# The values' last conv pieces done later and by the vector engine alone, and a thirteenth seven-product group, in a hybrid mixer layer

## The chip, the core and the metric

The kernel runs on one core of a Trainium2 chip. The metric is the device time of one execution in microseconds: the median of three runs. A profiled execution is a further one, with its own time. The engines are PE (TensorE, matrix products), DVE (VectorE), ACT (ScalarE), POOL (GpSimd, which here mostly issues transfers) and SP (SyncE, which here issues the weights' transfers). Each engine works through its own list of instructions in order and meets the others only at semaphores.

## The reference, cut to what matters

One layer: x of 256 tokens by 4096 is normed and multiplied by one large matrix; the columns of the product feed three mixers, and a second matrix takes the mixers' output back to 4096 columns.

```python
h = rms_norm(x, norm_g)
proj = einsum('bsd,dn->bsn', h, w_in)        # 4096 x about 13000
(aq, ak, av, ai, af, ao, az, bcq, bk, bv, bki, bwi, bz, cqkv, cb, ca, cz) = split(proj)
y_a = ...                                     # chunked mLSTM
y_b = ...                                     # sparse attention
qkv = silu(causal_depthwise_conv(cqkv, d_conv_w))   # 3072 channels, 4 taps
q_c, k_c, v_c = split(qkv, 3)
q_c, k_c = l2_normalize(q_c), l2_normalize(k_c)     # v_c is not normed
y_c = ...                                     # gated delta rule on q_c, k_c, v_c
x = x + einsum('bsm,md->bsd', concat(y_a, y_b, y_c), w_out)
```

The change concerns the six blocks of 512 columns of `cqkv` (the conv columns): their matrix product, the conv and silu behind it, and the move of `v_c` into another layout.

## The kernel before, in words

**Chunks.** The weights are streamed in 536 chunks, numbered in the order in which PE takes them; a chunk holds two row blocks of 128 of one block of 512 columns. fp32 products are made of three fp32r products: every weight tile is split into a high part (ACT, `split_hi`, L1626) and a low part (DVE, `split_lo`, L2021), and PE multiplies high by high, high by low and low by high. A plain chunk is 2 row blocks x 2 token halves x 3 = 12 matmuls of 512 columns. ACT and DVE work three chunks ahead of PE (`AHEAD`); there are four buffers for raw and four for split weights. SP issues the transfer of chunk c when DVE is through with the low part of chunk c-4 (`weights`, L874); for the second chunk of a group (below) it waits for the group's sums instead.

**Seven-product groups.** Conv columns 2 to 5 are worked in two pairs of column blocks (kind `cpair`). For some row-block pairs (`SEVEN`, token `S` in `CONV_ORDER`) the 2x2 block product is made with seven products instead of eight: PE does 6 matmuls in the first chunk (`seven_first`) and 15 in the second (`seven_second`), 21 instead of 24. In exchange DVE makes four sums of raw weights (`seven_sums`, L2031 to L2036), and splits them (ACT L1624, DVE `seven_lo` L2045, two halves). The activations' own sums are made beforehand (`xs`, `xh`, `xl`), one set per row-block pair in `X_S`. When a pair's groups are through, `evs` (DVE, four additions), `evx` (ACT, scaling) and `evn` (DVE, once per column block) bring the seven results together.

**Slots.** A planner (`plan`, L129) lists beside each chunk the pieces of other work that every engine does right after that chunk's own work: the slot. An engine whose list has a piece in slot c does it after its part for chunk c (DVE and ACT: after the split of chunk c+3), in the order in which the planner put pieces into that slot. The pieces that matter here:

- `cd` i (DVE, L2237): turns a conv piece (two of the 24 blocks of 128 channels) after POOL has moved its 32x32 blocks through DRAM (L993, L999), which POOL starts after `evn`; `conv` i: the first tap is a scaled copy on ACT (L1734), the other three taps are six multiply-adds on DVE (L2248); `csil` i (ACT, L1741): the silu. `CONV_SLOTS` gives the slots of the three. Pieces 0 to 7 are queries and keys, 8 to 11 the values.
- `csq` i: ACT squares a piece of queries or keys and splits it (L1747, L1750), DVE makes the low part (L2262); `cn` i: PE sums it over channels with two matmuls (L1379, L1380), waiting for the DVE part; `ce` i: ACT makes the scale, DVE applies it (L2270, L2272). ACT's `csq` waits for all twelve silus.
- `g1` to `g4`, `gb`: the gates' row work, on ACT and DVE (L2173 to L2199), read by PE in slot 130.
- `vd` (DVE, L2258): turns the values after POOL has moved them through DRAM (L1010, L1015). Before, POOL does this right after the conv moves and DVE turns them in slots 133 and 135.
- `cl` (DVE, slots 155 to 191): a triangular solve in lanes, whose operands POOL loads just ahead of it (L1054, L1058).

The last `cpair` chunk is 95; chunks 96 to 111 are the gates' columns, and so on.

Of the kernel before, what the change touches and what calls it, by code (L numbers as in the profile page):

```python
# [16 lines left out]
ALU = mybir.AluOpType  # L17
# [3 lines left out]
P = 128  # L21
D = 4096
SEQ = 256
M = SEQ // P
# [66 lines left out]
def lane_steps():  # L91

    pieces, spent = {}, 0
    for j in range(BLK - 1, 0, -1):
# [12 lines left out]
            [15, 8, 4, 9, 5, 10, 6, 11, 7, 12, 0, 13, 1, 14, 2, 3]]  # L107
SEVEN = [[0, 1, 2, 3, 4, 5], [0, 1, 2, 3, 4, 5],
         [8, 9, 10, 11, 12, 13], [8, 9, 10, 11, 12, 13, 14], [8, 9, 10, 11, 12, 13, 14]]
Y_S = [8, 9, 10, 11, 12, 13, 14]  # L110
OUT_PAIRS = range(2, 5)
CONV_SINGLE = 2
CONV_ORDER = ["12S1111S11S1122S22S22S1222", "12S11S11S11S11S22S12222222"]
X_S = [0, 1, 2, 3, 4, 5]
CONV_SLOTS = [(33, 34, 35), (35, 37, 39), (38, 43, 45), (46, 51, 53), (72, 78, 79), (75, 87, 89),
              (80, 91, 91), (82, 94, 94), (97, 99, 100), (99, 104, 105), (104, 105, 107), (106, 108, 109)]
CSQ_FROM = 110
PAIR_SLOTS = [(59, 60, 62, 63), (88, 89, 89, 97)]
S_PIECES = [(8, 10, 11), (9, 18, 23), (12, 25, 28), (17, 26, 30), (18, 34, 42), (25, 40, 44), (46, 47, 54)]
# [9 lines left out]
def plan():  # L129
# [77 lines left out]
    def weave(at, pieces, every=1):  # L207

        for piece in pieces:
            woven[at] += [] if piece is None else piece if isinstance(piece, list) else [piece]  # L210
            at += every
        return at
# [33 lines left out]
    at = max(weave(at + 1, [("ce", i) for i in range(8)]), g_end)  # L246
    weave(g_end + 1, [("vd", 0), ("vd", 1)], 2)
    weave(at + 4, [("kn", 0), ("kr", 0), ("kd", 0), ("kx", 0)], 3)
# [65 lines left out]
def hybrid_kernel(nc, x, norm_g, w_in, w_out, m_ib, m_fb, m_norm_g, a_cq_g, a_wuq, a_wuqi, a_qn_g, a_kn_g,  # L314
# [13 lines left out]
    with ExitStack() as ctx:  # L328
# [611 lines left out]
        def _(pool):  # L940
# [65 lines left out]

            pool.wait_ge(conv_ready, 12)
            for hg in range(2):
                for i in range(4):
                    pool.dma_start(v_dram[hg].rearrange("a f j i b -> i a (f j) b")[i],  # L1010
                                   v_heads(hg)[32 * i:32 * i + 32].rearrange("p (f b) -> p f b", b=32)
                                   ).then_inc(v_kept, 16)
                pool.wait_ge(v_kept, 16 * 4 * (hg + 1))
                for j in range(4):
                    pool.dma_start(v_heads(hg)[32 * j:32 * j + 32].rearrange("p (f c) -> p f c", c=P),  # L1015
                                   v_dram[hg][:, :, j].rearrange("a f i b -> a f (i b)")).then_inc(v_moved[hg], 16)

            wait_read(pool, "cn", 7)
# [38 lines left out]
            for g in range(LANE_G):  # L1057
                pool.dma_start(lane_left[lane_part(g)].rearrange("p r c -> p (r c)"),  # L1058
                               lane_left_dram[:].rearrange("m s k r c -> (m s k) (r c)")
                               ).then_inc(lane_left_loaded, 16)  # L1060
            pool.wait_ge(v_kept, 16 * 8 * M)
            for j in range(4):
# [535 lines left out]
        def _(act):  # L1598
# [129 lines left out]

            def conv(i, use):
                wait_read(act, "par", 0, 1)  # L1730
                act.wait_ge(conv_turned, i + 1)
                for j in range(2):
                    c = 2 * i + j
                    ins = func(cT[:, c, :], conv_columns(i, j), ACT.Copy,  # L1734
                               scale=par[:, R_N + 3 * CH + c:R_N + 3 * CH + c + 1])
                ins.then_inc(conv_y, 1)
# [6 lines left out]
            def csq(i, use):  # L1743
                act.wait_ge(conv_ready, 12)
                if i >= 2:
# [254 lines left out]
        def _(dve):  # L2000
# [241 lines left out]
            def conv(i, use):  # L2242
                dve.wait_ge(conv_y, i + 1)
                for d in range(1, CONV_K):
# [420 lines left out]
```

## Time and profile before

| | us |
|---|---|
| median of 3 runs | 1515.25 (1514.6 to 1515.85) |
| profiled execution | 1515.99 |
| its span, first to last instruction | 1514.1 |
| PE busy in it | 1509.8 |
| DVE busy | 1138.6 |
| ACT busy | 821.5 |
| POOL busy | 367.0 |

The profile's page gives busy time by engine, the groups of instructions, the chain of work that ended last and the transfers. The trace behind it can be asked for every instruction of a stretch (the timeline, with the idle time of the engine before an instruction in brackets and what ended it), for the waits of an engine, for the busy time in given stretches (windows) and for a stretch of the chain. Times are counted from the span's start. Matmuls are pipelined and the end of each is modelled, so the distance from one start to the next tells PE's pace, and not the duration given.

### The profile page before, as it was taken

The numbers are of one execution on the slowest core, as the hardware profiler recorded it, in microseconds if no ns is written. First come the engines' busy times: TensorE is split into PE (matmuls) and PEld (weight loads), VectorE is DVE, ScalarE is ACT, GpSimd is POOL, SyncE is SP. The second block draws the span as 40 slices with busy tenths as digits, with TensorE's granted clock in tenths as the row PEclk, the third lists the DMA queues.
The fourth block names the chain that finished last, engine by engine and source line by source line (L and its number), as shares of the span: only waits on it lengthen the run. The fifth ranks groups of instructions, "written<-read, shape, count | busy, mean of one in ns | idle before, by whom it ended". The sixth has DMA issues, their size and how long they took to land.

```text
span 1514.1 us, 19057 instructions
## 1 busy us (share of the span) xinstructions
PE 1509.8 (100%) x6900; PEld 1249.9 (83%) x6900; DVE 1138.6 (75%) x1712; ACT 821.5 (54%) x1100; POOL 367.0 (24%) x612
## 2 busy tenths in 40 slices
PE   9999999999999999999999999999999999999999
PEld 7888888888888887888878888888888888888887
DVE  6889899847769855576579676676557789988894
ACT  6766656587533444554545545544345656555563
POOL 9040131330230040126420254344400112000101
PEclk9999999999999999999999999999999999999999
DMA  9876677976788775558765787798875667696867
GB/s 288 283 238 218 198 250 209 254 225 195 223 252 267 235 221 165 158 184 271 248 203 167 231 248 205 241 277 241 236 244 158 216 217 221 205 263 210 237 228 187
DMA packets 209070, 341.47 MB, mean 226 GB/s; under 512 B 53161, under 2 KB 60632, under 8 KB 208720
## 3 DMA queue, kind: packets, MB, share of 16 engines
q1 hardware_dynamic: 184784, 288.66, 61.2%
q0 software_dynamic: 24144, 51.57, 13.1%
q8 instruction: 55, 0.90, 0.2%
q14 instruction: 39, 0.32, 0.1%
q10 hardware_dynamic: 48, 0.02, 0.0%
HBM read 312.81 MB, written 30.83 MB: 227 GB/s over the span
## 4 chain that ended last, share of the span: by engine, by line
PE 98%; DVE 1%; ACT 0%; issue 0%; DMA 0%; DVEq 0%
PE acc L1289 25%; PE acc L1292 25%; PE acc L1291 25%; PE mix L1292 2%; PE mix L1291 2%; PE mix L1289 2%; PE mix L1305 2%; PE mix L1307 2%; PE mix L1306 2%; PE acc L1305 2%; PE acc L1307 2%; PE acc L1306 2%; PE mix L1398 1%; PE mix L1481 1%; PE mix L1470 0%; PE mix L1391 0%
## 5 line engine op out<-in xcount | busy, mean ns | idle before, releaser
L2021 DVE TENSOR_TENSOR w_lo<-w_raw,w_hi 128x1024 fp32r<-128x1024 f32 (+1 forms) x503 | 604.0, 1216 | 252.8 <-ACT w_hi L1626 247.9
L1626 ACT ACTIVATE w_hi<-w_raw 128x1024 fp32r<-128x1024 f32 (+1 forms) x503 | 522.5, 1049 | 371.8 <-PE acc L1292 277.3
L1289 PE MATMUL acc<-w_hi,op_hi 128*128 128x512 f32 (+1 forms) x1628 | 640.4, 393 | 0.3 <-DVE w_lo L2021 0.3
L1292 PE MATMUL acc<-w_hi,op_lo 128*128 128x512 f32 (+1 forms) x1628 | 633.4, 389 | 0.0
L1291 PE MATMUL acc<-w_lo,op_hi 128*128 128x512 f32 (+1 forms) x1628 | 633.3, 389 | 0.0
L1289 PEld LDWEIGHTS acc<-w_hi,op_hi 128*128 128x128 f32 x1628 | 305.7, 188 | 64.7 <-issue 1.3
L1292 PEld LDWEIGHTS acc<-w_hi,op_lo 128*128 128x128 f32 x1628 | 305.6, 188 | 63.8
L1291 PEld LDWEIGHTS acc<-w_lo,op_hi 128*128 128x128 f32 x1628 | 305.8, 188 | 61.9
L993 POOL DMA_DIRECT2D conv_dram<-y x48 | 30.7, 703 | 165.6 <-DVE y L2112 118.4
L1289 PE MATMUL mix<-w_hi,op_hi 128*128 128x512 f32 (+1 forms) x154 | 59.7, 388 | 0.0
L1291 PE MATMUL mix<-w_lo,op_hi 128*128 128x512 f32 (+1 forms) x154 | 59.7, 388 | 0.0
L1292 PE MATMUL mix<-w_hi,op_lo 128*128 128x512 f32 (+1 forms) x154 | 59.7, 388 | 0.0
L1624 ACT ACTIVATE t_hi<-t_raw 128x1024 fp32r<-128x1024 f32 x40 | 42.2, 1060 | 16.1 <-DVE t_raw L2031 10.2
L1154 POOL DMA_DIRECT2D bp_dram<-b_ps x48 | 31.4, 701 | 71.7 <-ACT b_ps L1860 66.1
L2045 DVE TENSOR_TENSOR t_lo<-t_raw,t_hi 128x1024 fp32r<-128x1024 f32 x40 | 47.0, 1218 | 0.0
L1617 ACT ACTIVATE w_hi<-w_raw 128x512 fp32r<-128x512 f32 x32 | 20.2, 632 | 48.8 <-PE mix L1307 21.5
L993 POOL DMA_DIRECT2D y_dram<-y x32 | 21.0, 831 | 98.3 <-DVE y L2367 68.6
L1860 ACT ACTIVATE b_ps<-b_s,st 128x128 f32<-128x128 f32 (+1 forms) x32 | 14.3, 446 | 45.6 <-DVE st L2488 45.6
L993 POOL DMA_DIRECT2D bq_dram<-qs x32 | 20.5, 712 | 74.2 <-DVE qs L2415 74.2
L1165 POOL DMA_DIRECT2D b_pT<-bp_dram x48 | 26.4, 566 | 35.7 <-DMA bp_dram<-b_ps 35.7
L1226 POOL DMA_DIRECT2D out_dram<-sum x4 | 4.8, 1443 | 120.6 <-DVE sum L2100 120.6
L1291 PEld LDWEIGHTS mix<-w_lo,op_hi 128*128 128x128 f32 x154 | 28.9, 188 | 6.0
(566 smaller groups left out, 1798.8 us busy)
## 6 DMA issues: line engine op xcount, KB each, us to landing
w_raw<-in_w_in_dram SPq DMA_DIRECT2D x367, 512.0 KB, 4.5
w_raw<-in_w_out_dram SPq DMA_DIRECT2D x128, 512.0 KB, 4.7
w_raw<-in_w_in_dram SPq DMA_DIRECT2D x16, 384.0 KB, 3.8
w_raw<-in_a_wuq_dram SPq DMA_DIRECT2D x12, 512.0 KB, 5.8
out_dram<-acc POOLq DMA_DIRECT2D x8, 512.0 KB, 7.0
out_dram<-in_x_dram POOLq DMA_DIRECT2D x7, 512.0 KB, 6.3
conv_dram<-y POOLq DMA_DIRECT2D x48, 64.0 KB, 4.0
y<-conv_dram POOLq DMA_DIRECT2D x48, 64.0 KB, 4.3
```

The costliest lines, as they stand in the source:

```text
L993: pool.dma_start(*kept_block(dst, src, m, i)).then_inc(signal, 16)
L1154: pool.dma_start(bp_dram[n % 2][:, :, :, i, :].rearrange("a k j b -> a (k j) b"), b_ps[32 * i:32 * i + 32, n % 2].rearrange("p (f b) -> p ...
L1289: nc.tensor.matmul(o, hi[:, kt, tok], hv[:, i, n0:n1], start=(kt == (kts if late else blk["kts"])[0]), stop=False)
L1291: nc.tensor.matmul(o, hi[:, kt, tok], lv[:, i, n0:n1], start=False, stop=False)
L1292: last_mm = nc.tensor.matmul(o, lo[:, kt, tok], hv[:, i, n0:n1], start=False, stop=(kt == blk["kts"][-1]))
L1305: nc.tensor.matmul(o, x_hi, w_hi_, start=start, stop=False)
L1306: nc.tensor.matmul(o, x_hi, w_lo_, start=False, stop=False)
L1307: return nc.tensor.matmul(o, x_lo, w_hi_, start=False, stop=stop)
L1624: func(halves(sum_hi)[:, half], sums[:, half], ACT.Copy).then_inc(t_hi_ready, 1)
L1626: func(split_ap(w_hi, c), w_raw[:, c % RAW_BUFS, 0:n], ACT.Copy).then_inc(hi_ready, 1)
L2021: vec.tensor_tensor(split_ap(w_lo, c), w_raw[:, c % RAW_BUFS, 0:n], split_ap(w_hi, c).bitcast(F32), ALU.subtract).then_inc(lo_ready, 1)
L2045: vec.tensor_tensor(halves(sum_lo)[:, half], sums[:, half], halves(sum_hi)[:, half].bitcast(F32), ALU.subtract).then_inc(t_lo_ready, 1)
```

## The change

The diff does four things. Conv columns 4 and 5 get a seventh seven-product group (thirteen in the conv columns instead of twelve), with one more set of activation sums, and the order of the chunks of both pairs changes a little. The slots of the conv pieces move: queries and keys within slots 31 to 95, piece 8 to 104 to 107, and pieces 9, 10 and 11 to slots 113, 119 and 124, with their silus at 147, 149 and 151. For these three pieces (`DVE_TAPS`) the first tap, too, is done by DVE, as two scalings, and ACT has no tap; ACT's squares wait for eight silus instead of twelve. The values' move through DRAM goes behind POOL's loads for the lane solve, and its turn on DVE from slots 133 and 135 to 195 and 197 (`V_FROM`).

```diff
--- before.py
+++ after.py
@@ -105,17 +105,19 @@
 COPY_FROM, COPY_EVERY = 166, 3
 PAIR_KTS = [[4, 5, 6, 7, 8, 15, 9, 14, 10, 0, 11, 1, 12, 2, 13, 3], [15, 8, 4, 5, 9, 6, 10, 7, 11, 0, 12, 1, 13, 2, 14, 3],
             [15, 8, 4, 9, 5, 10, 6, 11, 7, 12, 0, 13, 1, 14, 2, 3]]
-SEVEN = [[0, 1, 2, 3, 4, 5], [0, 1, 2, 3, 4, 5],
+SEVEN = [[0, 1, 2, 3, 4, 5], [0, 1, 2, 3, 4, 5, 6],
          [8, 9, 10, 11, 12, 13], [8, 9, 10, 11, 12, 13, 14], [8, 9, 10, 11, 12, 13, 14]]
 Y_S = [8, 9, 10, 11, 12, 13, 14]
 OUT_PAIRS = range(2, 5)
 CONV_SINGLE = 2
-CONV_ORDER = ["12S1111S11S1122S22S22S1222", "12S11S11S11S11S22S12222222"]
-X_S = [0, 1, 2, 3, 4, 5]
-CONV_SLOTS = [(33, 34, 35), (35, 37, 39), (38, 43, 45), (46, 51, 53), (72, 78, 79), (75, 87, 89),
-              (80, 91, 91), (82, 94, 94), (97, 99, 100), (99, 104, 105), (104, 105, 107), (106, 108, 109)]
+CONV_ORDER = ["1211S11S11S1122S22S22S1222", "12S11S11S11S12S2222S22S12"]
+X_S = [0, 1, 2, 3, 4, 5, 6]
+CONV_SLOTS = [(31, 40, 41), (31, 43, 45), (42, 53, 55), (49, 57, 59), (71, 77, 79), (77, 81, 83),
+              (77, 85, 86), (86, 93, 95), (104, 106, 107), (109, 113, 147), (110, 119, 149), (112, 124, 151)]
 CSQ_FROM = 110
-PAIR_SLOTS = [(59, 60, 62, 63), (88, 89, 89, 97)]
+DVE_TAPS = 9
+V_FROM = 195
+PAIR_SLOTS = [(59, 61, 61, 64), (93, 94, 94, 97)]
 S_PIECES = [(8, 10, 11), (9, 18, 23), (12, 25, 28), (17, 26, 30), (18, 34, 42), (25, 40, 44), (46, 47, 54)]
 A_SLOTS = [(1, 4, 10), (7, 11, 18), (22, 27, 30), (34, 36, 41)]
 YD_SLOTS = [40, 43, 53, 62]
@@ -244,7 +246,7 @@
         at = weave(at, [([("csq", i)] if i < 8 else []) + ([("cn", i - 2)] if i > 1 else [])])
     g_end = weave(max(at, end("gates", 512) + 2), [(name, 0) for name in ("gt", "g1", "g2", "g3", "g4", "gb")], 2)
     at = max(weave(at + 1, [("ce", i) for i in range(8)]), g_end)
-    weave(g_end + 1, [("vd", 0), ("vd", 1)], 2)
+    weave(V_FROM, [("vd", 0), ("vd", 1)], 2)
     weave(at + 4, [("kn", 0), ("kr", 0), ("kd", 0), ("kx", 0)], 3)
     for u in range(len(UNITS)):
         at = weave(at, [("ca", u), None, ("cg", u), None])
@@ -1004,17 +1006,6 @@
                 pool.wait_ge(conv_kept, 16 * 4 * M * (j + 1))
                 bring_blocks(conv_stage(j), conv_dram[j % 2], brought[j % 2])
 
-            pool.wait_ge(conv_ready, 12)
-            for hg in range(2):
-                for i in range(4):
-                    pool.dma_start(v_dram[hg].rearrange("a f j i b -> i a (f j) b")[i],
-                                   v_heads(hg)[32 * i:32 * i + 32].rearrange("p (f b) -> p f b", b=32)
-                                   ).then_inc(v_kept, 16)
-                pool.wait_ge(v_kept, 16 * 4 * (hg + 1))
-                for j in range(4):
-                    pool.dma_start(v_heads(hg)[32 * j:32 * j + 32].rearrange("p (f c) -> p f c", c=P),
-                                   v_dram[hg][:, :, j].rearrange("a f i b -> a f (i b)")).then_inc(v_moved[hg], 16)
-
             wait_read(pool, "cn", 7)
             clear_corners(1)
 
@@ -1058,6 +1049,17 @@
                 pool.dma_start(lane_left[lane_part(g)].rearrange("p r c -> p (r c)"),
                                lane_left_dram[:].rearrange("m s k r c -> (m s k) (r c)")
                                ).then_inc(lane_left_loaded, 16)
+            pool.wait_ge(conv_ready, 12)
+            for hg in range(2):
+                for i in range(4):
+                    pool.dma_start(v_dram[hg].rearrange("a f j i b -> i a (f j) b")[i],
+                                   v_heads(hg)[32 * i:32 * i + 32].rearrange("p (f b) -> p f b", b=32)
+                                   ).then_inc(v_kept, 16)
+                pool.wait_ge(v_kept, 16 * 4 * (M + hg + 1))
+                for j in range(4):
+                    pool.dma_start(v_heads(hg)[32 * j:32 * j + 32].rearrange("p (f c) -> p f c", c=P),
+                                   v_dram[hg][:, :, j].rearrange("a f i b -> a f (i b)")).then_inc(v_moved[hg], 16)
+
             pool.wait_ge(v_kept, 16 * 8 * M)
             for j in range(4):
                 pool.dma_start(c_kt[32 * j:32 * j + 32],
@@ -1727,6 +1729,8 @@
                 func(gder[:, 2:4, :], gcol[:, 0:2, :], ACT.Exp).then_inc(g_cols, 1)
 
             def conv(i, use):
+                if i >= DVE_TAPS:
+                    return
                 wait_read(act, "par", 0, 1)
                 act.wait_ge(conv_turned, i + 1)
                 for j in range(2):
@@ -1741,7 +1745,7 @@
                 func(t, t, ACT.Silu).then_inc(conv_ready, 1)
 
             def csq(i, use):
-                act.wait_ge(conv_ready, 12)
+                act.wait_ge(conv_ready, 8)
                 if i >= 2:
                     act.wait_ge(c_sq_lo, i - 1)
                 step(func(c_square(i), cT[:, 2 * i:2 * i + 2, :].rearrange("p c t -> p (c t)"), ACT.Square))
@@ -2240,7 +2244,15 @@
                 vec.transpose(part, part).then_inc(conv_turned, 1)
 
             def conv(i, use):
-                dve.wait_ge(conv_y, i + 1)
+                if i < DVE_TAPS:
+                    dve.wait_ge(conv_y, i + 1)
+                else:
+                    dve.wait_ge(conv_turned, i + 1)
+                    for j in range(2):
+                        c = 2 * i + j
+                        row = R_N + (CONV_K - 1) * CH + c
+                        step(vec.tensor_scalar(cT[:, c, :], conv_columns(i, j), par[:, row:row + 1], None, ALU.mult),
+                             but=1 - j)
                 for d in range(1, CONV_K):
                     for j in range(2):
                         c = 2 * i + j
```

## Rows read from the trace of the kernel before

**Rows 1.** The page, part 1: busy us (share) and instructions by engine.

```profile
PE 1509.8 (100%) x6900; PEld 1249.9 (83%) x6900; DVE 1138.6 (75%) x1712; ACT 821.5 (54%) x1100; POOL 367.0 (24%) x612
```

**Rows 2.** Waits of PE, whole span: total us, times, longest.

```profile
PE acc L1289 <- DVE w_lo L2021: 0.3, 1, 0.3
```

**Rows 3.** Timeline of PE, 316.9 to 321: start us, us, what.

```profile
317.04 0.39 PE L1289 MATMUL acc<-w_hi,op_hi 128*128 128x512 f32 x1
...
319.76 0.39 PE L1379 MATMUL mix<-csq_hi,ones 128*128 128x512 f32 x1
```

**Rows 4.** Timeline of DVE, 234 to 240: work of one seven-product group.

```profile
234.44 1.22 DVE L2031 TENSOR_TENSOR y<-w_raw 128x1024 f32<-128x1024 f32 x1
...
237.02 0.69 DVE L2016 TENSOR_TENSOR w_lo<-w_raw,w_hi 128x512 fp32r<-128x512 f32 x1
237.62 2.36 DVE L2045 TENSOR_TENSOR tc_lo<-y,tc_hi 128x1024 fp32r<-128x1024 f32 x2
```

**Rows 5.** Timeline of DVE, 171 to 229 (idle time in brackets).

```profile
171.54 0.69 DVE L2097 TENSOR_TENSOR part_sum<-mix,y 128x512 f32<-128x512 f32 x1 [1.72 <-ACT y L1914]
...
177.74 2.36 DVE L2021 TENSOR_TENSOR w_lo<-w_raw,w_hi 128x1024 fp32r<-128x1024 f32 x2 [2.08 <-ACT w_hi L1626]
...
228.20 2.32 DVE L2045 TENSOR_TENSOR tc_lo<-y,tc_hi 128x1024 fp32r<-128x1024 f32 x2
```

**Rows 6.** Timeline of PE at 232.65: the first matmul of chunk 84.

```profile
232.65 0.39 PE L1289 MATMUL mix<-w_hi,op_hi 128*128 128x512 f32 x1
```

**Rows 7.** Windows: stretch, length, then busy us (instructions) by engine.

```profile
187.00:264.00 77.00, 77.00 (x341) 63.74 (x341) 72.62 (x89) 45.56 (x54) 19.45 (x34) 1.00 0.76 232
413.00:437.00 24.00, 24.00 (x108) 19.94 (x107) 14.15 (x16) 10.17 (x10) 12.74 (x25) 1.00 0.85 238
540.00:560.00 20.00, 20.00 (x90) 16.57 (x89) 9.80 (x8) 8.41 (x9) 9.12 (x12) 1.00 0.90 248
```

**Rows 8.** Timeline of DVE: taps, one-source scalings, value transposes.

```profile
299.18 2.45 DVE L2248 SCALAR_TENSOR_TENSOR cT<-y,par,cT 128x255 f32<-128x255 f32 x6
...
344.90 0.27 DVE L2173 TENSOR_SCALAR rows<-rows 8x256 f32<-8x256 f32 x1
...
377.74 1.30 DVE L2258 STREAM_TRANSPOSE cT<-cT 128x512 f32<-128x512 f32 x2
...
415.03 0.54 DVE L2233 TENSOR_SCALAR kiT<-mix,par 128x256 f32<-128x256 f32 x1
```

**Rows 9.** Timeline of DVE at 316.89: fourth squared piece's low part.

```profile
316.89 0.69 DVE L2262 TENSOR_TENSOR csq_lo<-kv,csq_hi 128x512 fp32r<-128x512 f32 x1
```

**Rows 10.** Timeline of DVE, 349 to 352.3: slot 124.

```profile
349.67 1.21 DVE L2021 TENSOR_TENSOR w_lo<-w_raw,w_hi 128x1024 fp32r<-128x1024 f32 x1
...
351.56 0.69 DVE L2270 SCALAR_TENSOR_TENSOR cT<-cT,c_vk 128x512 f32<-128x512 f32 x1 [0.68 <-ACT c_vk L1758]
```

**Rows 11.** Chain that ended last, 352 to 361.5: start us, us, what.

```profile
352.51 1.22 DVE w_lo L2021
...
354.33 1.14 DVE w_lo L2021
...
360.30 1.15 DVE w_lo L2021
...
361.49 0.50 PE acc L1289
```

**Rows 12.** The page, part 6: weight transfers, KB each, us to landing.

```profile
w_raw<-in_w_in_dram SPq DMA_DIRECT2D x367, 512.0 KB, 4.5
```

**Rows 13.** DMA issues, 300 to 326, with the values' moves under way.

```profile
w_raw<-in_w_in_dram SPq DMA_DIRECT2D x8, 512.0 KB, 4.6
```

**Rows 14.** DMA issues, 425 to 450, lane solve's loads under way.

```profile
w_raw<-in_w_in_dram SPq DMA_DIRECT2D x8, 512.0 KB, 8.1
```

**Rows 15.** Timelines of DVE and PE, 440 to 446: chunk 158.

```profile
442.63 1.22 DVE L2021 TENSOR_TENSOR w_lo<-w_raw,w_hi 128x1024 fp32r<-128x1024 f32 x1 [5.04 <-ACT w_hi L1626]
...
445.89 0.39 PE L1289 MATMUL acc<-w_hi,op_hi 128*128 128x512 f32 x1
```

## The prediction

> **What bounds the kernel now.** I read the page's busy times first: PE is busy 1509.8 us of a span of 1514.1, DVE 1138.6 [rows 1]. Since a matmul's end is modelled, the second view is PE's timeline: from one chunk's first matmul at 317.04 to the work behind it at 319.76 lie 2.72 us for 12 matmuls, 0.227 us each, and this pace holds nearly throughout [rows 3]. The third view is what PE waits for: behind the start there is one wait, 0.3 us for a low part of the weights [rows 2]. So PE is the bound, at its own pace, and a change can do two things: alter the number of matmuls, or make PE wait. PE waits when DVE or ACT delivers a chunk's split, or a piece that PE needs, later than PE gets there. The fourth view is therefore where DVE is nearly full. From 187 to 264 (the second pair of conv columns) it is busy 72.62 of 77 us [rows 7]; and from 352.5 to 361.45 the chain that ended last runs through DVE without a break, up to the low part of chunk 130, for which PE waits [rows 11]. The chain's rows say: there, every microsecond more on DVE is a microsecond more at the end.
>
> **The change part by part.**
>
> The thirteenth group takes away 24 matmuls and adds 21: 3 x 0.227 = 0.68 us less on PE, the whole gain. On DVE a group costs the sums, 237.02 - 234.44 = 2.58 us; a half split, 237.62 - 237.02 = 0.60; and the low parts of the sums, 2 x 1.14 = 2.28, each as long as a split, against one full split of 1.14 that falls away [rows 4, 11]: 4.3 us more on an engine with 77 - 72.62 = 4.4 idle in that stretch [rows 7]. Is there room? In the first pair's end DVE idles 1.72 us before its additions, and then 2.08 before chunk 64's split, because ACT scales before it splits [rows 5]. The new slots put that scaling one slot later, so that DVE splits chunk 64 while ACT scales. Running DVE's list on from there, with one more conv piece ahead of the additions, I get the low parts of the group at chunk 83 to start at 226.8 instead of 228.20 [rows 5]. From 226.8: low parts to 229.1, split 84 to 230.2, six taps (now in slot 81) to 232.6, split 85 to 233.75. Chunk 89's weights are issued then and land 4.5 us later [rows 12], at 238.3; the sums end at 240.9, six taps at 243.3, the half split at 243.9, a turn (half of a pair's 1.30 [rows 8]) at 244.55, the first low half at 245.75. PE: chunk 84 starts at 232.65 [rows 6]; four plain chunks (10.88), six matmuls of the group's first chunk (1.36) and three of its second (0.68) bring it to 245.57. It waits 0.2 us. By the same walk chunks 47, 90, 97 and 98 have 0.5 to 1.1 us to spare, the additions of the second pair included. Bounds: no wait at all, and 1.5 us (rival two). I take 0.2.
>
> The extra activation sums (slots 29 to 31) are six short DVE operations, which I put at a group's sums and a half split, 3.2 us. The first group now begins at chunk 36 instead of 34, and two plain chunks leave DVE 2 x (2.72 - 1.14) = 3.2 us [rows 3, 11]. Hidden; at worst 0.5 us.
>
> A conv piece wholly on DVE is six taps, 2.45 us, and two scalings of 256 elements from SBUF. The trace has no such scaling of 128 partitions; the nearest rows are 0.27 us (256 elements, 8 partitions, SBUF) and 0.54 (128 partitions, but out of PSUM) [rows 8]. I take 0.27, the row with the same memory: 3.0 us a piece, and 3.5 as the upper bound.
>
> Against that choice I set a rule. The Trainium skill (VectorE: DVE Perf Modes, sections on Mode 2×_2P and on why PSUM operands drop a tier) says that an fp32 op with one tensor source runs two elements a cycle in SBUF and loses that with PSUM. By it the 0.54 is no model for the tap, as I assumed; were it one, the sum below would be 1.1 us higher.
>
> Slot 113 holds piece 9 ahead of the fourth squared piece on DVE. The latter starts at 316.89 today, right behind chunk 116's split, which waits for ACT [rows 9]. Queued behind 3.0 us of taps it starts at 319.9 and ends at 320.6. PE wants it in slot 115, when chunk 115 is through, at 319.76 [rows 3]: a wait of 0.85 us. (All in times of before; PE's own shift carries ACT and DVE along there, since they wait for its buffers.) Behind it are queued split 117, which DVE then makes at 320.6 to 321.8, before PE can have done chunk 116 (2.72 behind the wait), and on ACT the sixth piece's square, two slots on. Bounds: 0.5 to 1.4.
>
> Slot 119 holds piece 10. DVE waits for ACT both before and after it there (slots 119 to 121), so I put it at nothing; without that cover it costs its 3.0.
>
> Slot 124 holds piece 11, ahead of `ce3` on DVE. Chunk 127's split starts at 349.67 and takes 1.14, so DVE is free at 350.81; today it idles 0.68 us until ACT hands over `ce3` at 351.56 [rows 10]. The taps end at 353.8, `ce3` at 354.4, and split 128 starts then instead of at 352.51: 1.9 us late, the 3.0 less what the two waits for ACT swallow. From there the chain has no gap [rows 11], and the gates' row work lies in it: split 130 ends 1.9 us later than 361.45, and PE, already waiting for it today, waits 1.9 more. Bounds 1.5 to 2.4. DVE stays that much later until its idle time after 365; POOL's transfers of the gates' rows move with it, as PE does.
>
> ACT loses three pairs of taps and its silus move into 147 to 151, after an exponential, so a table load goes with the first; slot 207's silu then needs none. ACT is busy 10.17 of 24 us there [rows 7]: nothing. Without that cover each silu would cost its length.
>
> The values' move: POOL now issues it behind the lane solve's loads and no longer ahead of the corners' clearing and the gates' rows. Queued behind it on POOL are four loads for slot 209 and copies that wait for chunk 166's split, both late enough for its two round trips. The turns cost DVE 1.30 us a pair [rows 8], and at 195 and 197 DVE is busy 9.8 of 20 us [rows 7]: nothing either way, since PE does not wait at 133 to 135 today. Without cover, 2.6 us. What the transfers do to the weights is rival three.
>
> Sum: -0.68 + 0.2 + 0.85 + 1.9 = +2.27 us. Against the profiled execution (1515.99, of which the span is 1514.1) that is 1518.3; against the median of the runs, 0.74 lower, 1517.5. I forecast **1517.5**, 0.15% over before. About 0.2% (3.0 us) is what a measurement of this kernel can tell from no change, so this counts as no change, close to its edge.
>
> **The rivals.**
>
> One: the taps find room. If the scalings and taps pack tighter, or the two waits are swallowed by leads that I read too small, only the gain is left: 1515.25 - 0.68 = 1514.6; with half the waits, 1515.9. For it: ACT has less to do in 97 to 111. Against it: the wait at 361.49 is there already [rows 11], and DVE's order is fixed.
>
> Two: the second pair is full. Chunk 89's sums wait for its weights, and from there DVE has no idle time up to chunk 90. Place: PE in chunk 89. Price: all that the landing takes over 4.5 us; at 6 us it is 1.5 us, the sum +3.8, **1519.0**, slower. It decides from a landing of about 5.3 us (0.76 more makes 3.0). For it: under the lane loads a landing takes 8.1 us [rows 14], under the values' moves 4.6 [rows 13]. Against it: POOL moves nothing at that time.
>
> Three: the values' move jams the weights of chunks 158 to 161. Today transfers there take 8.1 us in the median [rows 14], chunk 158's low part ends at 443.85, PE starts it at 445.89 [rows 15]: 2.0 us are left. The moves put 0.5 MB in the place of another 0.5 MB and then three more batches over the next 20 us. If the landing of 158 grows by 4 us, PE waits 2: **1519.5**. It costs from 2.0 us of growth on. Against it: with these same moves under way at 300 to 326 a landing took 4.6, one tenth over the usual 4.5 [rows 12, 13].
>
> The Trainium skill (DMA: Bandwidth & Descriptors, section Issuing engines are not separate DMA queues) has all issuers' transfers on the same 16 DMA engines, interleaved, which is what rival three would need; the 8.1 us agree with it.
>
> That the change doesn't do what it says has no place: the matmuls are counted off by the code.
>
> **How the numbers follow.** Forecast 0.55 (its own range 1516.6 to 1518.8: the bounds of its terms), rival one 0.17, two 0.16, three 0.12. The range reaches down to 1515.1, halfway into rival one, and up to 1519.6, over two and most of three. Faster by over 0.2% (under 1512.2) has no mechanism: PE has no wait to lose but 0.5 us; 0.01. Slower (over 1518.28): rivals two and three, 0.28, and about a sixth of the forecast, 0.09; 0.37. The same: 0.62.
>
> **What would show it.** Right: PE 3 matmuls shorter; a gap of some 0.9 us in PE ahead of the two norm matmuls behind chunk 115, and of some 2.4 (0.5 today) ahead of chunk 130, with DVE named as the releaser of both; 8 DVE instructions of 3.0 us in slots 113, 119, 124; no gap at chunk 89 over 0.5, none at 158 to 166. Wrong: no gap at 115 or 130 (rival one), a gap in the second group chunk that waits on tc_lo (two), splits waiting for weights after 440 (three), or DVE scalings of 0.5 us.

## The result, and the profile after

The changed kernel takes 1519.02 us (median of 8 runs) and the kernel before 1515.18 in the same set: a ratio of 1.0025, with a 95% interval from 1.0016 to 1.0034. A second set of ten runs (E0 below) gave 1518.66 against 1515.46, 1.0021 with an interval from 1.0012 to 1.0031. The change makes the kernel 3.2 to 3.8 us slower. That lies on the edge of what counts as no change here (about 0.2%), and more likely just past it.

The profiled execution of after took 1520.24 us, of which the span is 1518.4. The page's first part answers to [rows 1]:

```profile
PE 1510.9 (100%) x6897; PEld 1249.0 (82%) x6897; DVE 1146.4 (75%) x1729; ACT 821.4 (54%) x1097; POOL 368.1 (24%) x612
```

The window of the second conv pair answers to [rows 7]:

```profile
187.00:264.00 77.00, 76.24 (x336) 62.52 (x335) 72.48 (x89) 45.38 (x55) 13.60 (x24) 1.00 0.73 220
```

PE has three matmuls fewer (6897 for 6900), so the group does what it says. In the second pair's stretch PE is no longer busy all the time (76.24 of 77). The view of PE's waits over the whole span, with the total, how often, and the longest, answers to [rows 2]:

```profile
PE acc L1291 <- DVE w_lo L2025: 1.9, 1, 1.9
PE mix L1560 <- DVE kv L2615: 1.1, 1, 1.1
PE acc L1307 <- DVE tc_lo L2049: 0.8, 1, 0.8
PE mix L1381 <- DVE csq_lo L2274: 0.7, 1, 0.7
PE mix L1307 <- DVE t_lo L2049: 0.2, 1, 0.2
```

The second of them belongs to the start and is in before's trace as well. The others are new or have grown, and DVE is the releaser of every one. From here on I measure a wait from start to start on PE's timeline, less the 0.227 us of a matmul at full pace; the bracket in a row leaves out part of it.

The fourth row is the norm matmuls behind chunk 115, against [rows 3, 9]. PE's timeline:

```profile
319.08 0.39 PE L1294 MATMUL acc<-w_hi,op_lo 128*128 128x512 f32 x1
320.16 0.50 PE L1381 MATMUL mix<-csq_hi,ones 128*128 128x512 f32 x1 [0.69 <-DVE csq_lo L2274]
```

1.08 - 0.23 = 0.85 us. DVE's timeline shows why:

```profile
316.40 0.61 DVE L2254 TENSOR_SCALAR cT<-y,par 128x256 f32<-128x256 f32 x2
317.04 2.46 DVE L2260 SCALAR_TENSOR_TENSOR cT<-y,par,cT 128x255 f32<-128x255 f32 x6
319.42 0.68 DVE L2274 TENSOR_TENSOR csq_lo<-kv,csq_hi 128x512 fp32r<-128x512 f32 x1
```

Piece 9 takes 3.02 us from its first scaling to the squared piece, and the squared piece that ran at 316.89 before now starts at 319.42.

The first row is chunk 130, against [rows 10, 11]. PE's timeline, from its last matmul of chunk 129:

```profile
361.62 0.39 PE L1294 MATMUL acc<-w_hi,op_lo 128*128 128x512 f32 x1
363.92 0.50 PE L1291 MATMUL acc<-w_hi,op_hi 128*128 128x512 f32 x1 [1.91 <-DVE w_lo L2025]
```

The chain that ended last runs from slot 124 to it on DVE alone:

```profile
351.40 0.54 DVE cT L2254 x2
...
351.96 2.46 DVE cT L2260 x6
354.42 0.60 DVE cT L2282
355.02 1.14 DVE w_lo L2025
...
362.73 1.15 DVE w_lo L2025
...
363.92 0.50 PE acc L1291
```

The wait is 2.30 - 0.23 = 2.07 us, where before had 0.48 (from 360.78 to 361.49). Another 0.2 us stands ahead of chunk 128.

Behind that wait comes what I had not foreseen. PE's timeline:

```profile
365.25 0.63 PE L1294 MATMUL acc<-w_hi,op_lo 128*128 128x512 f32 x1
365.68 0.63 PE L1291 MATMUL acc<-w_hi,op_hi 128*128 128x512 f32 x1
366.11 0.63 PE L1293 MATMUL acc<-w_lo,op_hi 128*128 128x512 f32 x1
```

The window of the same stretch, after and then before, with the granted clock third from the right (0.64 and 1.00):

```profile
364.00:368.00 4.00, 4.00 (x12) 2.97 (x12) 4.00 (x5) 1.00 (x2) 2.97 (x4) 0.64 0.71 154
...
364.00:368.00 4.00, 4.00 (x25) 3.13 (x24) 2.91 (x6) 1.59 (x3) 1.63 (x3) 1.00 0.84 217
```

From 365.25 to 367.81 the matmuls start 0.427 us apart instead of 0.227: PE runs at the lower of its two levels, 1.2 GHz. The row counts 12 matmuls in these 4 us. From chunk 130's first matmul to chunk 131's are 5.17 us (363.92 to 369.09), 1.6 more than in before (361.49 to 365.08).

The third row is the group of chunk 89, against [rows 4, 6], first in PE's timeline:

```profile
231.63 0.39 PE L1291 MATMUL mix<-w_hi,op_hi 128*128 128x512 f32 x1
...
244.52 0.40 PE L1309 MATMUL mix<-w_hi,s_more 128*128 128x512 f32 x1
245.68 0.50 PE L1307 MATMUL acc<-tc_hi,s_more 128*128 128x512 f32 x1 [0.76 <-DVE tc_lo L2049]
```

Then in DVE's:

```profile
238.25 1.23 DVE L2035 TENSOR_TENSOR y<-w_raw 128x1024 f32<-128x1024 f32 x1 [0.51 <-DMA w_raw<-in_w_in_dram]
...
244.44 2.32 DVE L2049 TENSOR_TENSOR tc_lo<-y,tc_hi 128x1024 fp32r<-128x1024 f32 x2
```

PE waits 1.16 - 0.23 = 0.93 us there.

The lane solve's stretch, against [rows 14, 15]: the weight transfers in the view of DMA issues from 425 to 450.

```profile
w_raw<-in_w_in_dram SPq DMA_DIRECT2D x9, 512.0 KB, 8.1
```

Chunk 158's low part in DVE's timeline, from 445.84 to 447.07 (PE takes it at 449.89):

```profile
445.84 1.23 DVE L2025 TENSOR_TENSOR w_lo<-w_raw,w_hi 128x1024 fp32r<-128x1024 f32 x1 [4.25 <-ACT w_hi L1628]
```

The landing takes 8.1 us as it did, and 2.8 us are left for chunk 158, where 2.0 were.

### The profile page after: what moved, and what is told of

The parts are those of the page before. It is cut to its first block, busy times and chain, and to the rows that moved or that the text cites. A ratio compares the mean times of both kernels' runs of the same rounds, so it can differ in the third digit from the quotient of the medians.

```text
span 1518.4 us, 19065 instructions
## 1 busy us (share of the span) xinstructions
PE 1510.9 (100%) x6897; PEld 1249.0 (82%) x6897; DVE 1146.4 (75%) x1729; ACT 821.4 (54%) x1097; POOL 368.1 (24%) x612
## 4 chain that ended last, share of the span: by engine, by line
PE 91%; DVE 5%; DMA 2%; ACT 1%; issue 1%; SPq 0%; ACTq 0%; DVEq 0%
PE acc L1291 25%; PE acc L1293 25%; PE acc L1294 25%; PE mix L1307 1%; PE mix L1309 1%; PE mix L1308 1%; DVE w_lo L2025 1%; PE mix L1293 1%; PE mix L1291 1%; PE mix L1294 1%; PE acc L1307 1%; PE acc L1308 1%; PE acc L1309 1%; PE mix L1400 1%; DVE cT L2260 1%; PE mix L1483 1%
## 5 line engine op out<-in xcount | busy, mean ns | idle before, releaser
L1294 PE MATMUL mix<-w_hi,op_lo 128*128 128x512 f32 (+1 forms) x146 | 56.6, 388 | 0.0
L1293 PE MATMUL mix<-w_lo,op_hi 128*128 128x512 f32 (+1 forms) x146 | 56.6, 388 | 0.0
L1626 ACT ACTIVATE tc_hi<-y 128x1024 fp32r<-128x1024 f32 x26 | 27.6, 1062 | 16.4 <-DVE y L2035 11.3
```

The costliest lines, as they stand in the source:

```text
L1293: nc.tensor.matmul(o, hi[:, kt, tok], lv[:, i, n0:n1], start=False, stop=False)
L1294: last_mm = nc.tensor.matmul(o, lo[:, kt, tok], hv[:, i, n0:n1], start=False, stop=(kt == blk["kts"][-1]))
L1626: func(halves(sum_hi)[:, half], sums[:, half], ACT.Copy).then_inc(t_hi_ready, 1)
```

## The experiments

Each kernel was timed beside the kernel before on the same chip; E1 to E4 ran on one chip, E0 and E5 to E7 on a second, E8 to E10 on a third, E11 on a fourth. Medians in us, the ratio to before with its 95% interval:

| run | what | median | before | ratio | interval |
|---|---|---|---|---|---|
| E0 | the changed kernel again | 1518.66 | 1515.46 | 1.0021 | 1.0012 to 1.0031 |
| E1 | twelve groups | 1519.88 | 1515.80 | 1.0025 | 1.0015 to 1.0035 |
| E2 | late pieces in 118, 119, 120 | 1515.30 | 1515.80 | 0.9996 | 0.9987 to 1.0005 |
| E3 | in 113, 119, 120 | 1516.63 | 1515.80 | 1.0005 | 0.9996 to 1.0014 |
| E4 | in 118, 119, 124 | 1517.62 | 1515.80 | 1.0014 | 1.0005 to 1.0023 |
| E5 | ACT does the scalings | 1517.62 | 1515.46 | 1.0016 | 1.0007 to 1.0024 |
| E6 | E2, piece 6 later | 1515.57 | 1515.46 | 1.0001 | 0.9992 to 1.0010 |
| E7 | in 118, 123, 124 | 1521.13 | 1515.46 | 1.0040 | 1.0027 to 1.0054 |
| E8 | before, values' move late | 1514.64 | 1515.82 | 0.9994 | 0.9985 to 1.0003 |
| E9 | in 118, 126, 126 | 1523.74 | 1515.82 | 1.0050 | 1.0037 to 1.0062 |
| E10 | E2, key and value factors later | 1514.62 | 1515.82 | 0.9995 | 0.9986 to 1.0004 |
| E11 | E10 and E6 together | 1514.31 | 1515.80 | 0.9991 | 0.9982 to 1.0000 |

**E2, the late pieces where DVE is idle.** Theory: slots 113 and 124 are the cause of the loss. Rivals: the late silus and the values' move are; or the slow stretch has a cause of its own.

```diff
-              ... (109, 113, 147), (110, 119, 149), (112, 124, 151)]
+              ... (109, 118, 147), (110, 119, 149), (112, 120, 151)]
```

> The changed kernel with the taps of pieces 9, 10 and 11 in slots 118, 119 and 120, where its trace shows VectorE idle for 0.8 to 3.9 us at a time, and nothing else changed. My theory: all that the change lost behind chunk 112 comes from where pieces 9 and 11 stand. The 0.85 us at the norm matmuls behind chunk 115 goes, the wait ahead of chunk 130 falls from 2.07 to the 0.49 of before, and the stretch of matmuls 0.427 us apart behind it (364 to 368 us, 1.6 us lost) goes with it, since before had no such stretch there. Together 0.85 + 1.6 + 1.6 = 4.05 less: about 1515.0, within 0.2% of before. Rival one, that the slow stretch has nothing to do with the wait (it belongs to the place or to that execution): only 2.45 less, 1516.6. Rival two, that the late silus or the values' move cost the time: within 0.5 of the changed kernel, 1518.5 to 1519.5.

Measured: 1515.30, 0.5 below before, and all of PE's waits in the trace are these:

```profile
PE mix L1560 <- DVE kv L2615: 1.1, 1, 1.1
PE acc L1291 <- DVE w_lo L2025: 0.3, 1, 0.3
PE mix L1307 <- DVE t_lo L2049: 0.2, 1, 0.2
```

The waits behind chunk 115 and at chunk 128 are gone, that at chunk 130 is back at 0.49 (0.72 from start to start), and so is the granted clock at 1.00. The 3.2 to 3.8 us went with the slots of two pieces; silus at 147 to 151 and the values' move, which this kernel keeps, cost nothing that shows.

**E3 and E4, one of the two pieces at a time.**

```diff
E3:
+              ... (109, 113, 147), (110, 119, 149), (112, 120, 151)]
E4:
+              ... (109, 118, 147), (110, 119, 149), (112, 124, 151)]
```

> The changed kernel with piece 9's taps left in slot 113, piece 10's in 119 and piece 11's moved from 124 to 120. My theory: 0.85 us of wait ahead of the norm matmuls behind chunk 115 stays, the 2.07 us ahead of chunk 130 falls to 0.5 and the half-speed matmuls behind it go: 1519.0 - 1.6 - 1.6 = 1515.8. Rival, the half-speed stretch is not tied to the wait: 1517.4.

> The changed kernel with piece 9's taps moved from 113 to 118, piece 10's in 119, piece 11's left in 124. My theory: only the 0.85 us behind chunk 115 goes; about 2.1 us of wait ahead of chunk 130 stays, and so does the stretch behind it with matmuls 0.427 us apart, 1.6 us: about 1518.2, and 1515.8 + 1518.2 - 1515.0 is the changed kernel again if the two pieces' costs add. Rival, the slow stretch came of both waits together or of that execution: 1516.6.

Measured against E2 on the same chip: E3 is 1.33 above it (the theory had 0.8) and E4 2.32 (the theory had 3.2); together 3.65. The traces split them cleanly. E3's PE timeline has the one wait, 1.08 - 0.23 = 0.85 us again, and chunk 130's is at 0.48:

```profile
319.36 0.39 PE L1294 MATMUL acc<-w_hi,op_lo 128*128 128x512 f32 x1
320.44 0.50 PE L1381 MATMUL mix<-csq_hi,ones 128*128 128x512 f32 x1 [0.69 <-DVE csq_lo L2274]
```

E4's has the other, 2.31 - 0.23 = 2.08, with the slow stretch behind it in the profiled execution (granted clock 0.57 from 364 to 368):

```profile
360.44 0.39 PE L1294 MATMUL acc<-w_hi,op_lo 128*128 128x512 f32 x1
362.75 0.50 PE L1291 MATMUL acc<-w_hi,op_hi 128*128 128x512 f32 x1 [1.92 <-DVE w_lo L2025]
...
364.24 0.61 PE L1291 MATMUL acc<-w_hi,op_hi 128*128 128x512 f32 x1
364.65 0.63 PE L1293 MATMUL acc<-w_lo,op_hi 128*128 128x512 f32 x1
365.08 0.63 PE L1294 MATMUL acc<-w_hi,op_lo 128*128 128x512 f32 x1
```

But the slow stretch isn't in every execution. The mean granted clock was 0.999 in 2 of E4's 11 executions and 1.000 in the others. The median of those that read 1.000 is 1517.53, 2.2 above E2. The mean over a whole execution has three digits, so a fall that costs less than about half of the 1.6 us above would still read 1.000, and only a profiled execution shows where the clock fell. That the falls of the others lie behind chunk 130 too is concluded from the kernels: no execution reads below 1.000 without a wait of 2 us or more there.

**E1, twelve groups.** It isolates the group and asks whether that is what keeps chunk 89 waiting.

```diff
-SEVEN = [[0, 1, 2, 3, 4, 5], [0, 1, 2, 3, 4, 5, 6],
+SEVEN = [[0, 1, 2, 3, 4, 5], [0, 1, 2, 3, 4, 5],
-              "12S11S11S11S12S2222S22S12"]
+              "12S11S11S11S12S2222S221212"]
-X_S = [0, 1, 2, 3, 4, 5, 6]
+X_S = [0, 1, 2, 3, 4, 5]
```

> The changed kernel with the second conv pair back at six grouped pieces, slots and values' move as changed. My theory: the 13th group is worth its three matmuls, 3 x 0.227 = 0.68 us, and has no part in the wait ahead of chunk 89's group matmuls (0.93 us in the changed kernel's trace), since it lies behind it, in chunks 92 and 93. So PE gets three matmuls more, 6900, the 0.93 stays within 0.2, and the time is 0.7 us above the changed kernel, about 1519.7. Rival: the seventh group's sums and splits are what made VectorE late; then the 0.93 goes, and the time is 0.2 to 0.3 below the changed kernel's, about 1518.8.

Measured: 6900 matmuls, the wait at chunk 89 still there at 0.43, and 4.1 above before, where the changed kernel is 3.2 to 3.8 above. The sign fits, but the intervals overlap almost wholly: the group's 0.68 us is read off the count of matmuls, and the times can't confirm it. The wait at chunk 89 halved, where the theory had it unchanged; the account below shows why one execution can't settle that. This trace told something else. It has the same wait ahead of chunk 130, 2.27 - 0.23 = 2.04, and yet no slow stretch; the windows' row:

```profile
364.00:368.00 4.00, 3.94 (x23) 3.10 (x24) 4.00 (x6) 1.14 (x2) 2.84 (x4) 1.00 0.52 147
```

**E0, E5 and E7: when does the clock fall?** E0 is the changed kernel with no edit. E5 takes 0.6 us from each wait, E7 adds a second piece to the full stretch.

```diff
E5:
-DVE_TAPS = 9
+DVE_TAPS = 12
E7:
+              ... (109, 118, 147), (110, 123, 149), (112, 124, 151)]
```

> The changed kernel itself once more, beside the next three. The half-speed stretch behind chunk 130 shows up in some executions only: mean granted clock 0.999 in 3 of its first 8, in 4 of 8 of the twelve-group kernel, in 2 of 11 of the kernel with only piece 11 in slot 124, and in none of the 22 of the two kernels without piece 11 there. My theory: about 1519.0 where the clock stays at 1.0 and 1.2 to 1.6 more where it falls, in a third to a half of the executions; median 1519.2 to 1519.8. Rival, that the fall belonged to one chip: none here.

> The changed kernel with the first tap of pieces 9, 10 and 11 (the two scalings) on ScalarE, as for the other nine; the other six instructions stay on VectorE in slots 113, 119 and 124. The changed kernel's trace has the pair of scalings at 0.60 to 0.61 us of VectorE. My theory: each of the two waits shrinks by just that, 0.85 to 0.25 behind chunk 115 and 2.05 to 1.45 ahead of chunk 130, and the clock falls less often or not at all: the changed kernel less 1.2, about 1518.0. Rival: ScalarE, which is busy 9.5 of 10 us from 350 to 360, passes the delay on through its halves of the weights, and nothing or less than 0.5 is gained.

> The changed kernel with piece 9 in slot 118, piece 10's taps moved from 119 to 123 and piece 11's in 124: two pieces, 6.1 us of VectorE, in the full stretch in place of one. My theory: VectorE has no idle time from 341.4 on, so the second piece's 3.06 us goes to PE's wait ahead of chunks 127 to 130 in full: 2.1 becomes 5.1. Against the kernel with only piece 11 there (1517.5): 1520.6 without, and about 1522.1 with, the half-speed stretch. If the length of the wait is what lets the clock fall, it falls in all or nearly all of the executions, and the median is about 1522; rival, if it falls by some other condition, in two of eleven as there, and the median is about 1520.6.

Measured. E0: granted clock 0.999 in 4 of 10 executions, on another chip than E1 and E4, so the fall does not belong to one chip. Their median is 1519.5 and that of the others 1517.8, 1.2 below what the theory had. E5: the wait behind chunk 115 is down to 0.20 and that of chunk 130 to 1.97 - 0.23 = 1.74, with none left at 128; together these waits are 1.2 shorter than in E0's trace, so ACT had the room. No execution of 11 has a fallen clock. The median is 1.04 below E0, but only 0.2 below E0's executions that kept the clock, and E5's trace has 0.3 us more wait at chunk 89 than E0's: that the 1.2 us of these waits come back in the time isn't shown. E7: the second piece goes to PE in full, in three waits:

```profile
PE acc L1291 <- DVE w_lo L2025: 4.7, 3, 1.9
```

From start to start these are 1.09, 1.98 and 2.09 us ahead of chunks 127, 128 and 130, 5.2 in all; the median is 3.5 above E4's (another chip). The clock fell in 2 of 5 executions, the profiled one not among them: there my theory was wrong and the rival right. As far as five executions tell, it isn't the sum of the waiting that decides.

**E9, the same two pieces ahead of one wait.**

```diff
+              ... (109, 118, 147), (110, 126, 149), (112, 126, 151)]
```

> The changed kernel with piece 9 in slot 118 and the taps of pieces 10 and 11 both in slot 126, straight ahead of the halves of chunk 130 on VectorE. The kernel with these two pieces in slots 123 and 124 had the same extra work but three waits (1.1, 2.0 and 2.1 us ahead of chunks 127, 128 and 130), the half-speed stretch in two of five executions, and 1521.1. My theory: the same 5.1 us now stands in one wait ahead of chunk 130; if the length of a single wait is what lets the clock fall, it falls in every execution, and the median is 1521.1 + 1.3 = 1522.4. Rival: whether it falls hangs on something else than the wait's length, and it falls in a part of the executions as before: about 1521.1 to 1521.6.

Measured: 1523.74, 1.3 above the theory, and the clock fell in all five executions (0.997 or 0.998 in the mean). PE's timeline:

```profile
359.52 0.39 PE L1294 MATMUL acc<-w_hi,op_lo 128*128 128x512 f32 x1
366.26 0.80 PE L1291 MATMUL acc<-w_hi,op_hi 128*128 128x512 f32 x1 [6.35 <-DVE w_lo L2025]
366.86 0.63 PE L1293 MATMUL acc<-w_lo,op_hi 128*128 128x512 f32 x1
```

The windows, with the granted clock in the third column from the right:

```profile
360.00:364.00 4.00, 0.00 (x0) 0.00 (x0) 3.76 (x9) 0.56 (x2) 0.00 (x0) 0.78 0.00 0
364.00:368.00 4.00, 1.74 (x4) 1.45 (x5) 3.96 (x7) 2.83 (x4) 1.23 (x2) 0.50 0.23 31
368.00:372.00 4.00, 4.00 (x12) 2.67 (x12) 2.82 (x3) 0.00 (x0) 2.37 (x4) 0.50 0.81 218
```

PE stands still for 6.74 - 0.23 = 6.5 us, more than E7's 5.2 in all. The granted clock falls while it still waits (0.78 from 360 to 364), and all twelve matmuls of chunk 130 and the transposes behind it then run at 1.2 GHz. In E7 and here chunk 130 starts within 0.05 us of the same time (366.21, 366.26), and chunk 131 starts at 369.80 there and at 372.65 here. These 2.8 us are the clock alone, where the theory had 1.3.

**E6, piece 6 behind chunk 89's halves.**

```diff
-              ... (77, 85, 86), (86, 93, 95),
+              ... (77, 87, 88), (88, 93, 95),
```
(on top of E2)

> The kernel with the three late pieces in slots 118, 119 and 120, and besides piece 6's taps moved from slot 85 to 87 and its silu and the turn of piece 7 to 88, so that they stand on VectorE behind the grouped halves of chunk 89. The wait for these halves was 0.93 in the changed kernel's profiled execution, 0.43 with twelve groups, 0.47 with piece 9 alone in 113, and none in the two others: it hangs on the execution. My theory: it was piece 6's 2.45 us ahead of the halves; no execution waits there now, and the mean falls by 0.2 to 0.5 against the kernel without this move, to about 1515.0, 0.4 to 0.8 below the kernel before. Rival: the taps now make the weights of chunks 90 and 91 late, and the same wait stands there: no gain, 1515.3 to 1515.8.

Measured: no wait at chunk 89 in the trace, but 1515.57 and a ratio of 1.0001, no gain that the times show. E2's own profiled execution has no wait there either, so this run alone settles little; what it adds stands under **Chunk 89** below.

**E8, the values' move alone, in the kernel before.**

```diff
-    weave(g_end + 1, [("vd", 0), ("vd", 1)], 2)
+    weave(195, [("vd", 0), ("vd", 1)], 2)
```
(and POOL's two round trips moved, as in the change)

> The kernel before, with one part of the change alone: the values' move, its turns on VectorE at 195 and 197 and its sixteen DMAs on GpSimd behind the keeping of the other units. My theory: the move costs nothing, neither where it was nor where it is: no wait of PE at chunks 158 to 166, and within 0.4 us of the kernel before. Rival: the move is what makes the two waits of 0.3 us at the grouped halves of the output blocks, near 1434 us, which the changed kernel's traces show and that of before doesn't: then 0.3 to 0.6 above before.

Measured: 1514.64, 1.2 below before with an interval that includes no change. No wait at 158 to 166. The wait near 1434 us is 0.22, and before has 0.18 there by the same measure, so the move doesn't make it; E1, which has the late move as well, has none. What sets it stays open. Nor does the move gain the 1.2 us. In the profiled executions E8's span is 1.4 us shorter than before's (1512.7 and 1514.1), and this lies in the start: PE begins its first plain chunk at 16.19 in E8 and at 17.65 in before. From there to the end both take 1496.5.

**E10 and E11, a better version.** E10 takes away the wait that before has, too; E11 adds E6's move.

```diff
-    at = max(weave(at + 1, [("ce", i) for i in range(8)]), g_end)
+    at = max(weave(at + 1, [("ce", i) for i in range(4)] + [None] * 2 + [("ce", i) for i in range(4, 8)]), g_end)
```
(on top of E2; E11 with E6's slots besides)

> The kernel with pieces 9, 10 and 11 in slots 118, 119 and 120, and besides the last four of the eight pieces of the key and value factors (0.67 us of VectorE each) moved two slots back, from 125 to 128 to 127 to 130, so that two of them come behind the halves of chunk 130. My theory: the 0.49 us wait ahead of chunk 130, which before has too, goes; the sum against before is then -0.68 for the group, -0.49 for the wait and +0.3 for the two waits near 1434 us, so about 0.9 below before. Rival: ScalarE's halves come no sooner than VectorE's (it waits for ScalarE at 350 us), and the wait stays: within 0.4 of before.

> The kernel with the three late pieces in slots 118 to 120 and the later key and value factors, and piece 6's taps in slot 87 with its silu and piece 7's turn in 88 besides: every wait of PE that the studies found between chunk 85 and chunk 131 is taken away. My theory: against before, -0.68 for three matmuls, -0.49 for the wait ahead of chunk 130, +0.2 to 0.5 for the waits near 1434 us: 0.7 to 1.0 below before, just what five rounds can tell from no change. Rival: what the sixth piece leaves at chunk 89 it gives back at 90 or 93, as the kernel with that move alone (ratio 1.0001) would have it: within 0.4 of before.

Measured: in E10 chunk 130's low part comes 0.8 us before PE wants it, and the wait is gone; 1514.62, 1.2 below before, the interval still holding 1. E11: no wait at chunks 89, 115, 128 or 130, but one of 0.3 at chunk 97 (266.53), as its rival had it in kind; 1514.31 against 1515.80, ratio 0.9991, the interval's upper end at 1.0000. It is the fastest median of the twelve. But E8, whose trace saves nothing, came out 1.2 below before as well. Counted from the first plain chunk (18.39 in E10, 17.36 in E11), the profiled executions of E10 and E11 are 0.4 and 0.3 us shorter than before's. So the named waits are shown gone; a gain of 0.3 to 0.4 us is seen in one execution of each, and the rest of the 1.2 and 1.5 us in the medians is not explained.

## Why the prediction was right, and where it was not

**The forecast** was 1517.5 with a range to 1519.6; the time was 1519.02, inside the range and 1.5 over the likeliest value. The mechanism was right: the group pays 0.68, and two pieces of taps on DVE cost more than that. That the number fell inside the range is in part luck: it lies above the forecast's own range (1516.6 to 1518.8), in the stretch that was opened for rivals two and three, and a cost that no rival named brought it there.

**The group** (-0.68): 6897 matmuls, as counted.

**Chunk 89** (+0.2 forecast) was mis-sized: 0.93 in the profiled execution. In the ten profiled executions with piece 6 in slot 85 the wait was 0, 0, 0.20, 0.36, 0.37, 0.43, 0.46, 0.49, 0.52 and 0.93, a mean of 0.38. With piece 6 in slot 87 (E6, E11) it was zero both times. PE's side doesn't make the difference: the changed kernel starts chunk 84 at 231.63 in after and at 231.66 in E0, where the wait is 0.20. DVE's side does. My walk had the first low half start 11.9 us behind chunk 84's first matmul; in E0 it is 11.88, in after 12.81 (244.44), in all ten 11.5 to 12.8. From 180.4 to 196.2 the DVE rows of after and E0 lie within 0.03 us of each other. Then DVE waits for ACT, first after, then E0:

```profile
198.44 1.23 DVE L2025 TENSOR_TENSOR w_lo<-w_raw,w_hi 128x1024 fp32r<-128x1024 f32 x1 [1.05 <-ACT w_hi L1628]
201.13 1.23 DVE L2025 TENSOR_TENSOR w_lo<-w_raw,w_hi 128x1024 fp32r<-128x1024 f32 x1 [1.46 <-ACT w_hi L1628]
...
197.90 1.23 DVE L2025 TENSOR_TENSOR w_lo<-w_raw,w_hi 128x1024 fp32r<-128x1024 f32 x1 [0.48 <-ACT w_hi L1628]
200.29 1.22 DVE L2025 TENSOR_TENSOR w_lo<-w_raw,w_hi 128x1024 fp32r<-128x1024 f32 x1 [1.16 <-ACT w_hi L1628]
```

ACT waits there for weights to land, 1.87 and 1.62 us in after and 1.35 and 1.32 in E0. Weights issued from 190 to 204 take 6.6 us (median) in after, 5.7 in E0 and 5.2 in E2, which has no wait at chunk 89; the usual time is 4.5 [rows 12]. From there to the sums (238.25 and 237.35) DVE has nothing left to make it up with. Over the ten executions the wait grows roughly with DVE's idle time from 185 to 214: 1.34 and 1.36 us where it is zero (E2, E4), 2.51 in after. POOL moves conv pieces through DRAM at that time; that its moves are what makes the weights late is not tested. The step that was mis-sized is thus the walk's DVE, which took no late weights into account.

**Piece 9 in slot 113** (+0.85): 0.85 in after and in E3, by the delay that was worked out; E3 is 1.33 above E2, and their intervals against before overlap, so the times fit 0.85 and don't measure it.

**The price of a piece** (3.0 us): 3.02. The pair of scalings, for which I had to choose between 0.27 and 0.54 each, takes 0.54 in the chain, 0.27 each. The Trainium skill's rule (VectorE: DVE Perf Modes, Mode 2×_2P) has one-source fp32 in SBUF at twice the pace. The trace agrees in direction: taken alone, a scaling lasts 0.34 us, and the same size out of PSUM 0.54; the factor of two itself can't be read off these rows.

**Piece 11 in slot 124** (+1.9): 1.6 at chunk 130 and 0.2 at chunk 128, 1.8 together. E4 fits it, 2.2 over E2 in executions with the clock kept.

**The terms put at nothing** (the extra activation sums, piece 10 in slot 119, ACT's silus, the values' turns) show no wait of PE in the view of its waits above.

**What was missing** is the clock, which the sum put at nothing and did not name. With a wait of 2.04 to 2.1 us ahead of chunk 130 the granted clock fell in 15 of 42 executions (3 of 8 in the first set, 4 of 10 in E0, 4 of 8 in E1, 2 of 11 in E4, 2 of 5 in E7). With 1.74 us (E5) it fell in none of 11, with 0.5 or none there (E2, E3, E6, E8, E10, E11) in none of 66, with 6.5 us (E9) in all 5. It costs 1.6 us in the profiled execution, and 1.2 to 1.7 between the medians of executions with and without it in the first set, E0, E1 and E4: on average 15/42 x 1.6 = 0.6. My sum counted a wait as its own length.

**The account**, with these sizes: -0.68 + 0.38 + 0.85 + 1.8 + 0.6, and 0.2 to 0.3 more than before near 1434 us, is 3.2 us. Behind a wait PE's second matmul starts 0.34 us after the first (363.92 and 364.26) instead of 0.227; three waits more than before make that 0.3, together 3.5 us. The two sets measured 3.8 and 3.2.

**The rivals.** One fell with the waits at 115 and 130. Two had the right place, and late weights do feed the wait, but those of chunks some 40 us earlier: of the weights issued from 232 to 236, chunk 89's among them, the median took 4.1 us. Three did not happen: 8.1 us a landing before and after, and no wait behind 440; E8 shows that the move alone costs nothing. The chances leaned to no change, with the forecast 0.8 us from the edge; 0.2 more at chunk 89, the clock's 0.6, 0.3 of slower starts behind waits and 0.2 to 0.3 near 1434 were enough to cross it.

## What to carry to other kernels

Work that moves to an engine with idle time on average belongs in the very slots where that engine's timeline shows the idle: the same three pieces cost 3 to 4 us in slots 113, 119 and 124 and nothing that shows in 118 to 120. Price a wait of the matrix engine with what may follow it: here the clock sometimes fell behind a wait of 2 us, which then cost 3.6. And where two engines meet with less than a microsecond to spare, look at several executions before giving the wait a size: two executions of the changed kernel differed by 0.7 us at one and the same wait. When traces are compared, set the start apart: PE began its first plain chunk anywhere from 16.19 to 18.39 us in the fourteen profiled executions.

## What the runs showed of the hardware

PE's clock fell to 1.2 GHz behind a single wait of 2.04 to 2.1 us in about a third of the executions of one and the same kernel, in none of 11 behind 1.74 us, in all five behind 6.5 us; with three waits of 1.1 to 2.1 us, each a few microseconds behind the last, it fell in two of five. What decides between the executions of one kernel stays open. At the lower level matmuls of 512 columns start 0.427 us apart, against 0.227 in the stretches around it. The Trainium skill (TensorE: Matmul & The Clock Gate, section Wait — 56ns, not 53.3ns?) gives 426.7 ns for the cold array at 512 columns, and the rows agree; its 215.7 ns for the warm one is below the 227 that this kernel's rows show.
